# Gelu, gate and diagonal for each gathered slot instead of each pair, and VectorE's row at every slot

## What is computed

```python
# x: 128 tokens at a time, n = rmsnorm(x); 8 heads x 16 chosen experts = 128 per token
u = jnp.take(u_tab, e, axis=0)            # e: chosen expert rows, out of 16384
act = jax.nn.gelu(jnp.einsum('nkd,nd->nk', u, xb), approximate=False) * gate
vv = jnp.take(v_tab, e, axis=0)
return jnp.einsum('nk,nkd->nd', act, vv)  # added to x, then the final norm
```

## Time and profile before

| | us |
|---|---|
| median of 3 runs | 2076.54 |
| profiled execution, its own time | 2083.81 |
| its span | 2082.0 |
| TensorE busy | 1644.7 |
| VectorE busy | 1404.9 |
| ScalarE busy | 842.1 |
| ScalarE: table loads at the Gelu line, 76 | 97.5 |
| ScalarE: Gelu on two columns, 272 | 55.4 |
| GpSimd busy, nearly all of it 544 gathers | 667.3 |
| mean DMA rate, GB/s | 348 |

### The profile page before, as it was taken

How to read it: one execution, slowest core, us unless ns; L and a number is a source line. 1 busy time by engine, 2 the same in 40 slices (tenths; PEclk the granted TensorE clock), 3 DMA queues, 4 the chain that set the end, 5 groups by cost and what they waited for, 6 DMA issues and landing times.

```text
span 2082.0 us, 30188 instructions
## 1 busy us (share of the span) xinstructions
PE 1644.7 (79%) x11118; PEld 1023.8 (49%) x11118; DVE 1404.9 (67%) x3158; ACT 842.1 (40%) x2477; POOL 667.3 (32%) x549
## 2 busy tenths in 40 slices
PE   8999999787877789999868667688897556555555
PEld 7888888553454567777544344354344211111110
DVE  5063511387877578889988369887778677667764
ACT  2533121244523485557646034464413333233342
POOL 0000000134332333322444134455433444444442
PEclk9999999888899999999998889887698877777777
DMA  6344334799999999999999999999999999999997
GB/s 231 101 151 128 97 111 147 278 375 416 393 414 385 401 415 337 401 386 358 409 403 420 414 358 397 397 405 365 374 419 418 420 405 421 421 421 421 421 396 295
DMA packets 128301, 724.80 MB, mean 348 GB/s; under 512 B 16480, under 2 KB 23392, under 8 KB 58016
## 3 DMA queue, kind: packets, MB, share of 16 engines
q0 software_dynamic: 78336, 570.46, 67.5%
q1 hardware_dynamic: 49200, 150.26, 19.9%
q10 hardware_dynamic: 624, 2.23, 0.3%
HBM read 713.85 MB, written 8.52 MB: 347 GB/s over the span
## 4 chain that ended last, share of the span: by engine, by line
PE 41%; DMA 29%; DVE 19%; ACT 6%; issue 3%; POOL 2%; DVEq 0%; ACTq 0%; POOLq 0%
DMA arena<-in_uv,arena 20%; PE ps L1076 8%; DVE arena L2010 7%; PE ps L1127 6%; PE ps L766 6%; PE ps L822 5%; DMA arena<-in_stream 4%; PE ps L994 3%; DMA arena<-in_w_out 2%; PE ps L1018 2%; POOL arena L1582 2%; DVE arena L1876 1%; DMA arena<-in_w_a 1%; DVE pos L1945 1%; DVE fin_odd L2025 1%
## 5 line engine op out<-in xcount | busy, mean ns | idle before, releaser
L1582 POOL DMA_INDIRECT arena<-in_uv,arena x544 | 666.2, 1225 | 1116.4 <-PE ps L1127 683.3
L2010 DVE CUSTOM_DVE_ANT_0 arena<-arena 128x1024 f32<-128x1024 f32 x544 | 659.7, 1222 | 256.2 <-DMA arena<-in_uv,arena 253.6
L1127 PE MATMUL ps<-arena 64*64 64x512 f32 (+1 forms) x3192 | 549.5, 759 | 236.5 <-ACT arena L1543 236.3
L1127 PEld LDWEIGHTS ps<-arena 64*64 64x64 f32 (+1 forms) x3192 | 120.5, 156 | 492.7 <-ACT arena L1543 386.2
L1557 ACT ACTIVATE gelu_d<-dots 128x2 f32<-128x2 f32 x272 | 55.4, 204 | 727.3 <-DVE dots L2010 726.8
L1076 PE MATMUL ps<-arena 128*128 128x294 f32 (+1 forms) x1152 | 293.8, 416 | 18.6 <-DMA arena<-in_stream 12.4
L1076 PEld LDWEIGHTS ps<-arena 128*128 128x128 f32 x1152 | 220.1, 192 | 95.0 <-DMA arena<-in_stream 17.4
L994 PE MATMUL ps<-arena 128*128 128x128 f32 (+1 forms) x1024 | 144.2, 303 | 34.0 <-DMA arena<-in_w_a 17.9
L994 PEld LDWEIGHTS ps<-arena 128*128 128x128 f32 x1024 | 136.2, 208 | 59.1 <-DMA arena<-in_w_a 19.5
L766 PE MATMUL ps<-arena 128*128 128x256 f32 x640 | 141.5, 384 | 3.5 <-DVE arena L1605 3.0
L1533 ACT ACTIVATE share<-gelu_d,arena 128x1 f32<-128x1 f32 x544 | 130.5, 287 | 10.9
(11 more groups left out here) (295 smaller groups left out, 1921.9 us busy)
## 6 DMA issues: line engine op xcount, KB each, us to landing
arena<-in_stream SPq DMA_DIRECT2D x144, 512.0 KB, 4.7
arena<-in_w_a SPq DMA_DIRECT2D x32, 512.0 KB, 9.4
arena<-in_w_out SPq DMA_DIRECT2D x32, 512.0 KB, 9.9
arena<-in_w_q SPq DMA_DIRECT2D x32, 512.0 KB, 7.6
arena<-in_uv,arena POOLq DMA_INDIRECT x544, 12.1
arena<-spill SPq DMA_DIRECT2D x2, 1920.0 KB, 14.0
arena<-in_x_prompt SPq DMA_DIRECT2D x4, 512.0 KB, 6.2
arena<-in_ln_g SPq DMA_DIRECT2D x4, 512.0 KB, 9.2
```

Source lines behind the costliest of these rows:

```text
L1127: mm = pe.matmul(ps[rows_out, half, :], diag[on_pe(k) % NDIAG][rows_in, 0:TS if t == NTILE else HALF_P], ring[k % SLOTS][rows_in, D + half ...
L1582: pool.indirect_dma_start(out=ring[kk % SLOTS], out_offset=None, in_=a["uv"], in_offset=bass.IndirectOffsetOnAxis(ap=idx[:, kk:kk + 1], ax ...
L2010: ins = dve.tensor_tensor_reduce(ring[s][:, 0:D], ring[s][:, 0:D], n2p if t == NTILE else n2[t % 2], 1.0, 0.0, ALU.mult, ALU.add, dots[k / ...
```

## The change

Gelu, the gate product and the diagonal are made for one slot, right after that slot's dot, on one column; `dot_ready`, `gelu_ready` and `share_ready` count slots and no longer pairs. VectorE adds its row (slot kk - 2) at every step kk. The buffers (`dots`, `gelu_d`, `share`, four of two columns) stay.

```diff
--- before.py
+++ after.py
@@ -740,7 +740,7 @@
                     sp.dma_start(x2, a["x_prompt"][(t + 1) * P:(t + 2) * P, :]).then_inc(xt_in, 16)
                 if kk == 3 * P + 1:
                     sp.wait_ge(n2_ready, norms(3))
-                    sp.wait_ge(dot_ready, 3 * P // 2)
+                    sp.wait_ge(dot_ready, 3 * P)
                     for q in range(QUARTERS):
                         sp.dma_start(n2p[q * TS:(q + 1) * TS, :], n2s[0:TS, :]).then_inc(packed, 16)
 
@@ -1524,24 +1524,22 @@
                 act.wait_ge(y_ready, t + 1)
                 act.dma_start(o["y"][t * P:t * P + rows(t), :], fins[t % 2][0:rows(t), :]).then_inc(y_out[t % 2], 16)
 
-            def diag_pair(u):
-                eye = fold[:, :] if 2 * u // P == NTILE else fold2
-                if u % (TOPK // 2) == 0:
-                    act.wait_ge(gate_ready, 2 * u // TOPK + 1)
-                act.wait_ge(gelu_ready, u + 1)
-                for j in range(2):
-                    ins = act.activation(share[u % 4][:, j:j + 1], gelu_d[u % 4][:, j:j + 1], ACT.Identity,
-                                         scale=gate[:, 2 * u + j:2 * u + j + 1])
-                ins.then_inc(share_ready, 1)
-                act.wait_ge(share_ready, u + 1)
-                for k in (2 * u, 2 * u + 1):
-                    if on_dve(k):
-                        continue
-                    n = on_pe(k)
-                    if n >= NDIAG:
-                        act.wait_ge(slot_free, n - NDIAG + 1)
-                    act.activation(diag[n % NDIAG][:, 0:eye.shape[1]], eye, ACT.Identity, scale=share[u % 4][:, k % 2:k % 2 + 1]
-                                   ).then_inc(diag_ready, 1)
+            def diagonal(k):
+                eye = fold[:, :] if k // P == NTILE else fold2
+                col, w = slice(k % 2, k % 2 + 1), share[k // 2 % 4]
+                if k % TOPK == 0:
+                    act.wait_ge(gate_ready, k // TOPK + 1)
+                act.wait_ge(gelu_ready, k + 1)
+                act.activation(w[:, col], gelu_d[k // 2 % 4][:, col], ACT.Identity, scale=gate[:, k:k + 1]
+                               ).then_inc(share_ready, 1)
+                if on_dve(k):
+                    return
+                act.wait_ge(share_ready, k + 1)
+                n = on_pe(k)
+                if n >= NDIAG:
+                    act.wait_ge(slot_free, n - NDIAG + 1)
+                act.activation(diag[n % NDIAG][:, 0:eye.shape[1]], eye, ACT.Identity, scale=w[:, col]
+                               ).then_inc(diag_ready, 1)
 
             flow = trunk(delta, tail, (rest(), second_sums(), second_lru()))
             flow.to(FIRST)
@@ -1551,11 +1549,11 @@
                 t, k = ends(kk)
                 if k == VLAG:
                     finish_sums(t)
-                if kk % 2 and kk < NS:
-                    u = kk // 2
-                    act.wait_ge(dot_ready, u + 1)
-                    act.activation(gelu_d[u % 4][:, :], dots[u % 4][:, :], ACT.Gelu).then_inc(gelu_ready, 1)
-                    diag_pair(u)
+                if kk < NS:
+                    col = slice(kk % 2, kk % 2 + 1)
+                    act.wait_ge(dot_ready, kk + 1)
+                    act.activation(gelu_d[kk // 2 % 4][:, col], dots[kk // 2 % 4][:, col], ACT.Gelu).then_inc(gelu_ready, 1)
+                    diagonal(kk)
                 flow.to(stage_at(kk))
                 for n in picks_at(kk - 1, 1):
                     pick_gates(n)
@@ -1850,7 +1848,7 @@
                 dve.wait_ge(n2_rcp, u + 1)
                 dve.wait_ge(chunk_in[c % RING], landed(c))
                 if u > 1:
-                    dve.wait_ge(dot_ready, (u - 1) * P // 2)
+                    dve.wait_ge(dot_ready, (u - 1) * P)
                 dve.scalar_tensor_tensor(out=n2[u % 2], in0=x2, scalar=rs2[:, u:u + 1], in1=wslot[c % RING],
                                          op0=ALU.mult, op1=ALU.mult).then_inc(n2_ready, 1)
                 if u == 3:
@@ -2009,13 +2007,12 @@
                 dve.wait_ge(row_in[s], uses(k // SLOTS + 1))
                 ins = dve.tensor_tensor_reduce(ring[s][:, 0:D], ring[s][:, 0:D], n2p if t == NTILE else n2[t % 2],
                                                1.0, 0.0, ALU.mult, ALU.add, dots[k // 2 % 4][:, k % 2:k % 2 + 1])
-                if k % 2:
-                    ins.then_inc(dot_ready, 1)
+                ins.then_inc(dot_ready, 1)
 
             def add_row(k):
                 t, fin = k // P, fins[k // P % 2]
                 v, w = ring[k % SLOTS][:, D:2 * D], share[k // 2 % 4][:, k % 2:k % 2 + 1]
-                dve.wait_ge(share_ready, k // 2 + 1)
+                dve.wait_ge(share_ready, k + 1)
                 if on_pe(k) - on_pe(t * P) == k - t * P:
                     if t > 1:
                         dve.wait_ge(y_out[t % 2], uses(t // 2))
@@ -2055,10 +2052,8 @@
                     join(t)
                 if kk < NS:
                     dot(kk)
-                if kk % 2 and 0 < kk // 2 <= NS // 2:
-                    for k in (kk - 3, kk - 2):
-                        if on_dve(k):
-                            add_row(k)
+                if VLAG <= kk < NS + VLAG and on_dve(kk - VLAG):
+                    add_row(kk - VLAG)
                 flow.to(stage_at(kk))
                 for n in picks_at(kk, 0):
                     made = pick_halves(n)
```

## The result

The changed kernel takes 2116.61 us in the median of 4 runs (2112.4 to 2124.63) against 2079.05 us before: 1.0179 times, with a 95% interval of 1.0146 to 1.0211. A second set of runs later gave 2123.09 us and 1.0196 (1.0162 to 1.0230). It is 37 to 43 us slower; the forecast was 2080 us.

A forecast was written before the change was run, and what follows sets the result against it. Gathered rows were taken to bound the DMA-full stretches, the trunk's products and convolutions 783 to 1001 us. Terms +7 + 0 + 0 - 2 - 2 = +3 on 2083.81; on the median's footing 2076.5 + 3.5, so 2080 us, range 2058 to 2104.

The forecast's parts named there:

- the outer gaps: About six gaps outside slots 95 to 160 that need extra table loads; counted, but given no cost.
- the first overrun: From 718 to 783 us ScalarE gets 76.2 us of work in 65, over by 11.2; costed 0, between 0 and 11.2.
- handling each slot singly: All 544 shares and 415 diagonals stay at the same cost each; only their place moves, no time added.
- the end: After the last dot four matmuls instead of eight, and about 0.25 us less on ScalarE: -2 us.
- The gathers rule outside 783 to 1001 us: In the DMA-full stretches gathered rows set the pace, 2.49 us a slot at 421 GB/s; trunk rules from 783 to 1001.
- The Silu stretch: From 911 to 1001 us, ScalarE over by 6.7 us in the last 46; costed +7, between 0 and 27.7.
- 64 loads, 2.77 us a gap: About 32 gaps on ScalarE each get two more table loads and a Gelu, 2.77 us; 82 us of loads in all.
- about 140: Sign in the changed kernel: about 140 table loads at the Gelu line, where 76 stood before.
- The wait at even slots: ScalarE's even-slot trunk work now stands behind that slot's dot; costed 0, between -11 and +11 us.
- VectorE's order: VectorE's 35 even rows come one slot earlier with no busy time changed; costed 0.
- The dips: Where queues run dry, even slots freed about one slot sooner: -2 us, between 0 and -29.
- The first slower rival: ScalarE becomes the bound from 718 to 1001 us, 97% of its idle time taken: +25, 2101 us; chance 0.19.

The follow-up runs named there:

- e10: Kernel before with semaphores counting slots, plus an extra constant Gelu without a wait in 26 gaps between slots 97 and 160 (47 loads): 2104.10 us, 1.0115.
- e11: Kernel before with semaphores counting slots, plus an extra constant Gelu without a wait only in the six gaps elsewhere (9 loads): 2100.35 us, 1.0086.
- e1: Kernel before, pairs kept, plus a Gelu of a constant at every even slot that waits for nothing (56 more loads): 2112.09 us, 1.0153.
- e4: Changed kernel, but 32 of 272 pairs keep one Gelu for both slots, so no load is added: 2090.03 us, 1.0060 against the kernel before.
- e5: Changed kernel with Identity in place of the dots' Gelu, slots handled singly (69 loads): 2087.10 us, 1.0035 against the kernel before.
- e6: Identity in place of the dots' Gelu, with pairs as in the kernel before (69 loads): 2076.08 us, 0.9985 against the kernel before.
- e2: Kernel before, but ScalarE also waits for each even slot's dot before that slot's trunk work; no load added: 2087.13 us, 1.0050.
- e3: Kernel before, but VectorE adds its row at every slot, two behind, while Gelu, shares and diagonals stay in pairs: 2087.36 us, 1.0039.
- e9: Control: kernel before with only the three semaphores counting slots, no instruction moved: 2087.42 us, 1.0042.

## Why the prediction was wrong

The step that failed is the price of nothing for ScalarE's added work wherever it was thought hidden: the outer gaps got no price, the first overrun got 0, and handling each slot singly got 0. The runs show about 9 to 13, 5 to 8 and 8 to 11 us in their place.

The sum of the parts that the runs give: loads 24 to 32 us (e10 and e11 make 24 by the ratios and 29.6 by the medians; e1's 33 less 1 to 4 for the place of its loads), single handling 8 to 11 (e4; e5 against e6), the end within the latter: 32 to 43, and 37 to 43 were measured. Point by point:

- *The gathers rule outside 783 to 1001 us, so that ScalarE's load elsewhere costs nothing.* **Here it failed first.** The text counted "about six more" gaps outside slots 95 to 160 and then gave them no price. e11 prices them at 9 to 13 us. A DMA share near 1 over a stretch of 300 us says that bytes flow, not that each link of the trunk has slack. In the heads of the delta stages exp, root and exp follow each other across ScalarE, VectorE and TensorE, every engine's slot work stands behind them in order, and the queues run dry within one such link (1195 to 1500 us had 383 GB/s, with dips; the text read this as a possible gain only).
- *The first overrun, 11.2 us, is taken back between 783 and 911 us.* Its size was right: 11.5 us more for slots 96 to 112. Part came back: the delay fell from 14.4 at slot 108 to 4.9 at slot 128. The kernel with the 47 loads alone shows 14.0 over the control at slot 108, 8.5 at slot 128. The wrong part was the path. The text asked how far ScalarE may fall behind TensorE's products (20 us), and these indeed hardly waited: from slot 112 to 160 TensorE idled 5.5 us ahead of them (1.9 before), ended by weights (3.8) and a convolution (1.6) and not by ScalarE. But VectorE waits for a share two slots back, and that reserve was gone: 11.8 us of waiting for shares from slot 96 to 112. The text named this path and put no price on it. Costed at 0 between 0 and 11.2, it was some 5 to 8.
- *The Silu stretch costs 7 us.* Slots 128 to 160 took 6.3 us more; in e10 3.7 over the control. Right.
- *64 loads, 2.77 us a gap.* There were 56, each of 1.283 us as in every row before. The 32 gaps were counted rightly, and each got one more load for its Gelu; but in 8 of them the two portions of trunk work needed different tables, so that the load to go back stood there already and only 24 were new. The text's sign of "about 140" loads at the Gelu line did not follow from its own sum, which puts 32 there, 108 in all, and 108 were found. ScalarE was expected at about 980 us and is at 1011.5, since the shares and diagonals lost the overlap of a pair, about 47 us, where the text said that only their place moves.
- *The wait at even slots, 0 between -11 and +11; VectorE's order, 0.* Both are 0 within the noise (e2, e3 against e9). But single handling as a whole is 8 to 11, which the text had nowhere: its share and diagonal stood at 0.
- *The dips, -2; the end, -2.* Slots freed earlier gained nothing anywhere that shows: GpSimd waits 742.3 us for TensorE where it was 683.3, and slots 224 to 332, which were to go faster if the dips closed, take 11.8 us longer. The end gave 2.2.

The first slower rival, ScalarE as the bound at 2101 us, had a chance of 0.19 and the right mechanism in two of its three stretches: ScalarE is the bound from slot 96 to 112, and the Silu overrun is there. Its terms for the dense stretch make 26.9 us, and e10 measured 15 to 17: the 9.0 us of reloads between them did not come. It too left out the outer gaps and the single handling. By the rule of "ScalarE: Activation LUTs" in the Trainium skill, section What ACT_TABLE_LOAD costs, a switch is 2.66 us with the drain, and the kernel would have come to 2155 us; the trace of the changed kernel again shows the Gelu 1.29 us after the start of its load (1029.91 and 1031.20), so the drain was not seen, and the loss is that of loads of 1.28 us in a chain.

## What to carry to other kernels

Where one engine's stream carries two kinds of work, a call of a function in another table costs a load for itself, and a second one to go back where the piece behind it needs the table of the piece before, as at 24 of the 32 places here; count the places before splitting a batch of two, and price each by the chain it stands in, not by the engine's busy share. A memory share near 1 over a long stretch hides short links where nothing has slack; a load of 1.28 us there cost 1.0 to 1.4 us of the whole kernel. And an experiment that regroups waits needs a control of its own, or it measures where the loads fell.

## What the runs showed that was not expected

The place of a table load against a wait matters: a Gelu that raises its semaphore by 2 and not by 1 went with loads that wait for the dot themselves, 39 of 76, and with 8 us (2087.4 against 2080), most of it between slots 224 and 286. And the loads of a batch of two were nearly free, 76 of them worth 3 us within an interval that holds none, while the next 56 cost 24 to 32.
